# First stage of a decoder step: memory values first, high halves and row sums on ScalarE, statistics through a diagonal, four shared weight slots

## The reference

```python
def _rmsnorm(x, g):
    xf = x.astype(jnp.float32)
    y = xf * lax.rsqrt(jnp.mean(xf * xf, axis=-1, keepdims=True) + RMS_EPS)
    return (y * g.astype(jnp.float32)).astype(x.dtype)

def _mem_kv(mem, g, w_k, w_v):
    n, m, _ = mem.shape
    hm = _rmsnorm(mem, g)
    return ((hm @ w_k).reshape(n, m, MEM_HEADS, MEM_HEAD_DIM),
            (hm @ w_v).reshape(n, m, MEM_HEADS, MEM_HEAD_DIM))
...
mkv = [_mem_kv(mem_prompt, norm_mem_kv[l], mem_w_k[l], mem_w_v[l]) for l in range(DEPTH)]
...
h = _rmsnorm(x, norm_mix[0])
u = h @ pool_w_in[0]
u_ext = u if pool_buf is None else jnp.concatenate([pool_buf[0], u], axis=1)
```

## Time and profile before

| what | value |
|---|---|
| median of three runs | 2504.84 us (2499.56 to 2507.42) |
| profiled execution, span on the core | 2500.6 us (no other total is given for it) |
| TensorE busy | 2411.1 us (96%) |
| VectorE, ScalarE, GpSimd busy | 1435.8, 820.9, 236.0 us |
| DMA | 433 MB, mean 173 GB/s |
| first matmul of `win` | 159.84 us |

### The profile page before, as it was taken

How to read it: one execution, slowest core, us unless ns; L and a number is a source line. 1 busy time by engine, 2 the same in 40 slices (tenths; PEclk the granted TensorE clock), 3 DMA queues, 4 the chain that set the end, 5 groups by cost and what they waited for, 6 DMA issues and landing times.

```text
span 2500.6 us, 45442 instructions
## 1 busy us (share of the span) xinstructions
PE 2411.1 (96%) x19126; PEld 2336.1 (93%) x19126; DVE 1435.8 (57%) x1419; ACT 820.9 (33%) x593; POOL 236.0 (9%) x230
## 2 busy tenths in 40 slices
PE   5989999899999999999999999998999999999998
PEld 5879997899999999999988997968999999999998
DVE  8587776755544554455655762847545445544555
ACT  3323433133333333333332332323333333333332
POOL 7040021200000000000201012312000000000002
PEclk7999999999999999999999999999999999999999
DMA  4745557155555556555445455454555555565553
GB/s 141 222 162 176 186 169 261 60 185 178 191 172 177 189 168 194 176 168 183 170 169 165 136 188 188 152 185 136 168 187 182 177 180 180 170 200 168 170 183 119
DMA packets 374185, 433.27 MB, mean 173 GB/s; under 512 B 7954, under 2 KB 340066, under 8 KB 373552
## 3 DMA queue, kind: packets, MB, share of 16 engines
q1 hardware_dynamic: 363632, 394.51, 48.2%
q0 software_dynamic: 10160, 36.83, 4.3%
q10 hardware_dynamic: 288, 0.43, 0.1%
HBM read 426.21 MB, written 6.45 MB: 173 GB/s over the span
## 4 chain that ended last, share of the span: by engine, by line
PE 54%; issue 34%; DVE 5%; POOLq 2%; DMA 2%; DVEq 2%; ACT 0%; POOL 0%; SPq 0%; ACTq 0%
PE acc L621 16%; PE acc L623 16%; PE acc L622 16%; DVE wlo L1075 1%; DVE xs L1113 1%; POOLq L1605 1%; PE acc L707 1%; POOLq L1600 1%; DVEq L1114 1%; PE ab L768 1%; DVE xs L1116 1%; PE ab L883 1%; DMA xs_flat<-in_cache_mem_k 1%; DMA raw<-in_mem_w_v 1%; PE acc L697 1%
## 5 line engine op out<-in xcount | busy, mean ns | idle before, releaser
L621 PE MATMUL acc<-xs,whi 128*128 128x264 f32 (+1 forms) x3712 | 1069.2, 288 | 37.2 <-DVE xs L1116 11.5
L623 PE MATMUL acc<-xs,wlo 128*128 128x264 f32 (+1 forms) x3712 | 1060.5, 286 | 0.0
L622 PE MATMUL acc<-xs,whi 128*128 128x264 f32 (+1 forms) x3712 | 1059.5, 285 | 0.0
L416 ACT ACTIVATE whi<-raw 128x2048 fp32r<-128x2048 f32 x372 | 706.9, 1913 | 1065.1 <-DMA raw<-in_ffn_w_up 304.0
L1075 DVE TENSOR_TENSOR wlo<-raw,whi 128x2048 fp32r<-128x2048 f32 x372 | 848.1, 2309 | 265.9 <-ACT whi L416 190.9
L621 PEld LDWEIGHTS acc<-xs,whi 128*128 128x128 f32 x3712 | 702.2, 189 | 41.0 <-issue 15.2
L623 PEld LDWEIGHTS acc<-xs,wlo 128*128 128x128 f32 x3712 | 706.5, 190 | 0.0
L622 PEld LDWEIGHTS acc<-xs,whi 128*128 128x128 f32 x3712 | 704.2, 190 | 0.2
L621 PE MATMUL acc<-hA,whi 128*128 128x264 f32 (+1 forms) x1216 | 350.2, 288 | 15.6 <-DVE x L1122 9.5
L623 PE MATMUL acc<-hA,wlo 128*128 128x264 f32 (+1 forms) x1216 | 348.6, 287 | 0.0
L622 PE MATMUL acc<-hA,whi 128*128 128x264 f32 (+1 forms) x1216 | 348.0, 286 | 0.0
(11 more groups left out here) (210 smaller groups left out, 1517.4 us busy)
## 6 DMA issues: line engine op xcount, KB each, us to landing
raw<-in_ffn_w_gate SPq DMA_DIRECT2D x88, 1024.0 KB, 5.3
raw<-in_ffn_w_up SPq DMA_DIRECT2D x88, 1024.0 KB, 5.2
raw<-in_ffn_w_down SPq DMA_DIRECT2D x88, 1024.0 KB, 5.4
raw<-in_dil_w_q SPq DMA_DIRECT2D x24, 1024.0 KB, 5.0
raw<-in_pool_w_in SPq DMA_DIRECT2D x16, 1024.0 KB, 5.5
raw<-in_pool_w_out SPq DMA_DIRECT2D x16, 1024.0 KB, 5.7
raw<-in_mem_w_k SPq DMA_DIRECT2D x8, 1024.0 KB, 5.3
raw<-in_mem_w_v SPq DMA_DIRECT2D x8, 1024.0 KB, 5.5
```

What stands on the lines that cost most here:

```text
L416: nc.scalar.activation(whi[:, n % NSPLIT, :], raw[:, n % 2, :], ACT.Copy).then_inc(hi_ready, 1)
L621: mm(out, w_hi, hi_, start=first, stop=False)
L622: mm(out, w_hi, lo_, start=False, stop=False)
L623: return mm(out, w_lo, hi_, start=False, stop=last)
```

## The change

What it does, part by part:

- Order of phases on TensorE: values of layer 0, then the transposes of token and state rows, keys 0, values 1, transposes of keys 0, keys 1, transposes of keys 1, `win`. In `value_phase` the loop over channel tiles is outside and the two token groups inside, so that a tile is used as soon as it is there.
- ScalarE makes the high halves of the normed inputs (`high_x`), VectorE only the low ones (`low_x`, `low_memory`). GpSimd makes none, and no squares before `wout`.
- ScalarE sums the squares of the memory and token rows as they lie, tokens on partitions (`rows_sum`). VectorE puts the sums on a diagonal (`diagonals`), and TensorE multiplies it by ones, which gives the sums along the free dimension (`row_statistics`).
- The transposed memory has a buffer of its own (`memT` in `kx`), no longer `x`. SP loads the token and state rows behind the first four blocks, into buffers outside `xs`; identity and gains are issued by ScalarE.
- `raw` has four slots and the low half is written over it in place (`wlo` is another name of the same memory). SP loads a block when TensorE has used the block four earlier. `hi` and `lo` no longer wait for that themselves.

```diff
-    ("memk0", 4, 2), ("memv0", 4, 1), ("memkt0", 0, 1),
-    ("memk1", 4, 2), ("xt", 0, 5), ("st", 0, 2), ("memv1", 4, 1), ("memkt1", 0, 1),
+    ("memv0", 4, 1), ("xt", 0, 5), ("st", 0, 2),
+    ("memk0", 4, 2), ("memv1", 4, 1), ("memkt0", 0, 1), ("memk1", 4, 2), ("memkt1", 0, 1),
...
-        raw = sb("raw", [P, 2, BLK])
         whi = sb("whi", [P, NSPLIT, BLK], F32R)
-        wlo = sb("wlo", [P, NSPLIT, BLK], F32R)
+        with nc.sbuf_tensor("wlo", [P, NSPLIT, BLK], F32R) as wlo:
+            pass
+        raw = sb("raw", [P, NSPLIT, BLK])
...
-                if n >= 2:
-                    eng.wait_ge(hi_ready, n - 1)
-                    eng.wait_ge(lo_ready, n - 1)
+                if n >= NSPLIT:
+                    eng.wait_ge(half_used, 2 * (n - NSPLIT + 1))
                 src = weight_source(n)
-                eng.dma_start(raw_as(n % 2, src.shape[1]), src).then_inc(raw_in[n % 2], 16)
+                eng.dma_start(raw_as(n % NSPLIT, src.shape[1]), src).then_inc(raw_in[n % NSPLIT], 16)
...
+                if n == NSPLIT:
+                    for key in (("x", 0), ("x", 1), ("x", 2), ("state", 0)):
+                        load_cached(eng, key)
...
                 landed(eng, n, more)
-                if n >= NSPLIT:
-                    eng.wait_ge(half_used, more * 2 + 2 * (n - NSPLIT + 1))
-                nc.scalar.activation(whi[:, n % NSPLIT, :], raw[:, n % 2, :], ACT.Copy).then_inc(hi_ready, 1)
+                nc.scalar.activation(whi[:, n % NSPLIT, :], raw[:, n % NSPLIT, :], ACT.Copy).then_inc(hi_ready, 1)
...
+            def rows_sum(key, c):
+
+                cached_landed(eng, key)
+                if c:
+                    eng.wait_ge(rows_summed, c)
+                nc.scalar.activation(ab[:, :, :].rearrange("p b c -> p (b c)"), cached(key), ACT.Square,
+                                     accum_out=ssqc[:, c:c + 1]).then_inc(rows_summed, 1)
+
+            def high_x(gen, m, src, width):
+
+                c = GAIN[gen[:-1]][0 if gen == "memkv0" else int(gen[-1])] + m
+                return nc.scalar.activation(xs[:, m, 0, 0:width], src, ACT.Copy, scale=gains[:, c:c + 1]).then_inc(xhi_ready, 1)
...
-            upto(1)
+            for c in range(2):
+                rows_sum(("mem", c), c)
+            hi(0)
+            at[0] = 1
             eng.wait_ge(acc_free, G0["xload"] + 1)
+            for m in range(DC):
+                high_x("memkv0", m, memT[:, m, :], TP)
+                if m % 4 == 3 and m < 12:
+                    upto(1 + m // 4)
...
+            root(STAT["mem"], TP)
+            eng.wait_ge(rows_summed, 2)
+            nc.scalar.activation(stdc[:, 0:2], ssqc[:, 0:2], ACT.Sqrt, bias=eps[:, :], scale=1.0 / D).then_inc(std_ready, 1)
+            upto(N0["memk0"])
             for m in range(DC):
...
-                if m % 8 == 3:
-                    upto(2 + m // 8)
-            root(STAT["mem"], TP, 2)
+            eng.wait_ge(std_ready, STAT["mem"] + 1)
+            for c in range(2):
+                rows_sum(("x", c), 2 + c)
+            upto(N0["memk0"] + 3)
+            upto(N0["memv1"])
+            eng.wait_ge(half_used, 2 * (N0["memk0"] + 4))
+            for m in range(DC):
+                high_x("mix0", m, x[:, m, :], T)
+                if m % 4 == 3 and m < 12:
+                    upto(N0["memv1"] + 1 + m // 4)
...
-                    for c in range(3 if samples else 2):
-                        out, t0, tn = (acc[:, 2 * (g % 2) + c, :], c * P, P) if c < 2 else (acc[0:TS, 2 * ((g + 1) % 2), :], TP, TS)
-                        for k in range(4):
+                    for k in range(4):
+                        if ready is not None:
+                            ready(4 * i + k)
+                        for c in range(3 if samples else 2):
+                            out, t0, tn = (acc[:, 2 * (g % 2) + c, :], c * P, P) if c < 2 else (acc[0:TS, 2 * ((g + 1) % 2), :], TP, TS)
...
-                        if c == 0 or c == (2 if samples else 1):
+                        if k % 2 == 1:
                             last.then_inc(half_used, 1)
...
+            def row_statistics(k, d, samples):
+
+                eng.wait_ge(diag_ready, d)
+                for c in range(2):
+                    last = mm(ab[:, 3, c * P:(c + 1) * P], ones[:, :], sq_flat[:, c * P:(c + 1) * P], start=True, stop=True)
...
-            pair_item(N0["memk0"], G0["memk0"], 2, xtile, xs_wait("memkv0"), width=TP)
-            statistics(STAT["mem"], TP, 2)
-            pair_item(N0["memk0"] + 2, G0["memk0"] + 1, 2, xtile, width=TP)
...
-            value_phase("memv0", False)
-            memory_keys_out(0)
-            pair_phase("memk1", 2, 2, htile, lambda k: eng.wait_ge(low_ready, k // 2 + 1), TP)
+            value_phase("memv0", False, None, xs_wait("memkv0"), lambda: row_statistics(STAT["mem"], 1, False))
...
-            value_phase("memv1", False, htile)
+            pair_phase("memk0", 2, 2, xtile, width=TP)
+            value_phase("memv1", False, htile, lambda k: eng.wait_ge(low_ready, k + 1))
+            memory_keys_out(0)
+            pair_phase("memk1", 2, 2, htile, width=TP)
             memory_keys_out(1)
-            pair_phase("win", 8, 2, xtile, xs_wait("mix0"), after_first=lambda: statistics(STAT["mix0"]))
+            pair_phase("win", 8, 2, xtile, xs_wait("mix0"), after_first=lambda: row_statistics(STAT["mix0"], 2, True))
...

-                landed(eng, n, more)
                 eng.wait_ge(hi_ready, more + (n + 1))
-                if n >= NSPLIT:
-                    eng.wait_ge(half_used, more * 2 + 2 * (n - NSPLIT + 1))
-                v.tensor_tensor(wlo[:, n % NSPLIT, :], raw[:, n % 2, :], whi[:, n % NSPLIT, :].bitcast(F32),
+                v.tensor_tensor(wlo[:, n % NSPLIT, :], raw[:, n % NSPLIT, :], whi[:, n % NSPLIT, :].bitcast(F32),
                                 ALU.subtract).then_inc(lo_ready, 1)
...
-            for m in range(0, DC, 2):
-                split_x(GAIN["memkv"][0], m, TP)
-                if m in (0, 6):
-                    upto(m // 6)
-            upto(3)
-            rms(STAT["mem"], TP, 2)
...
+            def low_x(gen, m, src, width):
+
+                c = GAIN[gen[:-1]][0 if gen == "memkv0" else int(gen[-1])] + m
+                eng.wait_ge(xhi_ready, 16 * XHI[gen] + m + 1)
+                v.scalar_tensor_tensor(out=xs[:, m, 1, 0:width], in0=src, scalar=gains[:, c:c + 1],
+                                       in1=xs[:, m, 0, 0:width].bitcast(F32), op0=ALU.mult, op1=ALU.subtract).then_inc(xs_ready, 1)
...
+            def diagonals(c0):
+
+                eng.wait_ge(rows_summed, c0 + 2)
+                for c in range(2):
+                    last = v.tensor_scalar(sq_flat[:, c * P:(c + 1) * P], ident[:, :], ssqc[:, c0 + c:c0 + c + 1], None, ALU.mult)
+                return last
...
+            eng.wait_ge(ident_in, 16)
+            lo(0)
+            at[0] = 1
+            for m in range(DC):
+                low_x("memkv0", m, memT[:, m, :], TP)
+                if m == 1:
+                    diagonals(0).then_inc(diag_ready, 1)
+                if m in (3, 7, 11):
+                    upto(1 + m // 4)
+            rms(STAT["mem"], TP, 2)
+            upto(N0["memk0"])
+            for m in range(10):
+                low_memory(m)
             memory_values(0)
-            upto(N0["memk1"] + 3)
-            memory_keys(1, N0["memv1"])
...
+            upto(N0["memk0"] + 1)
...
+            upto(N0["memk0"] + 2)
+            eng.wait_ge(stat_ready, STAT["mem"])
+            diagonals(2)
...
+            v.tensor_reduce(ssq[:, 0, 0:TS], squares.rearrange("p m b -> p b m"), AX.X, ALU.add).then_inc(diag_ready, 1)
+            for m in range(10, DC):
+                low_memory(m)
+            memory_keys(0, 0)
+            upto(N0["memk0"] + 3)
+            upto(N0["memv1"])
+            memory_keys(0, 1)
+            for m in range(DC):
+                low_x("mix0", m, x[:, m, :], T)
+                if m in (3, 7, 11):
+                    upto(N0["memv1"] + 1 + m // 4)
+            upto(N0["memk1"])
             memory_values(1)
+            upto(N0["memk1"] + 1)
+            memory_keys_staged(0)
...
-            squares(lambda j: taken(G0["memload"] + 3), TP)
-            taken(G0["xload"])
-            for m in range(0, DC, 2):
-                h, k, c = (hA, hB)[m // 8], m % 8, GAIN["memkv"][1] + m
...
-                eng.wait_ge(high_ready, m + 2)
-                gp.tensor_tensor(h[:, k:k + 2, 1, 0:TP], sq[:, :, 0:TP], h[:, k:k + 2, 0, 0:TP].bitcast(F32),
-                                 ALU.subtract).then_inc(low_ready, 1)
-                eng.drain()
-            load_cached(eng, ("x", 0))
-            load_cached(eng, ("x", 1))
-            eng.wait_ge(half_used, 2 * N0["memk1"])
-            for key in (("x", 2), ("state", 0)):
-                load_cached(eng, key)
-            squares(lambda j: taken(G0["xt"] + 4))
+            taken(G0["memkt0"])
```

(9 more changed lines are left out.)

123 lines of the change are left out of this document (69 added, 54 removed).

## The result

The kernel after takes 2457.83 us (median of 4, 2456.69 to 2459.17) against 2504.03 us (median of 4, 2499.56 to 2507.42) for the kernel before on the same chip: a ratio of 0.9821, 95% interval 0.9807 to 0.9835, so 46 us less. The forecast was 2468; its direction and main term held, and the time came out 10 us lower, 0.8 us above the lower end of the range of 2457 to 2487.

The account below looks back on a forecast made before the run. TensorE was taken as the bound, busy 2411.1 of 2500.6 us, with the first stage loose behind VectorE. The median 2504.84 less 37.1 us there, slots 0, gave 2467.7, say 2468; range 2457 to 2487.

Parts of the forecast that it names:

- main term: First stage, up to the first evacuation of the input projection: 137.3 us against 174.4, 37.1 us less.
- Start of the values: First values matmul on TensorE: at 18.0 us, not 20.8; 18.3 or 16.5 by other readings of DMA issue.
- Values of layer 0: First values phase: 22.4 us at full pace plus 2.5 for a slow clock spell and row statistics, ending at 42.9.
- Turning step: Transposing token and state rows between layer 0's values and keys: 10.0 us on VectorE, ending at 52.9.
- The ten megabytes of the sum: Data landing through the first keys block: 10 MB at 350 GB/s, landing near 33 us.
- rival A: Rows late: first keys block lands at 38 us, not 33, some 6 us lost, 2474 us; chance 0.20.
- Keys, values 1, keys 1: Rest of the first stage: keys 22.8 us each, values 22.4 + 0.3, input projection from 124.9, first evacuated at 137.3.
- GpSimd: First stage: losing its squares and second low halves gains nothing itself, but its absence allows VectorE's 2.29 and 0.45 us.
- Four slots: Weight loads in the loops: taken as 0; bounds 3 us gained and 6 us lost beside cache loads.
- From profile to median: Whole time: the three-run median lies 4.2 us above the profiled span, carried over to the forecast.
- Rival D: Better: start at 16.5 us, no slow clock spell, loops gain 3 us, 2461 us; chance 0.09.
- C: Slower: four slots make weights late in the steady loops, 2521 us at an excess of 0.6 us; chance 0.05.

Follow-up runs that it names:

- gains_on_sync: Kernel after, with the identity and seven gain rows issued by SyncE among the memory rows again, as before; 2459.68 us.
- pool_busy: Kernel after, with a hundred added multiplications of 384 columns on GpSimd from the start, ahead of the mask's load; 2474.94 us.
- layer1_first: Kernel after, with sixteen high and ten low tiles of the second layer's memory moved ahead of the first keys block; 2456.46 us, repeated 2454.79.
- after_again: Kernel after, unchanged, measured again beside later candidates on the same chip; 2457.18 us.
- slots_only: Kernel before, with the four shared weight slots alone; 2488.90 us, 0.9941 of before.
- two_raw_rest: Kernel after, with weight blocks from the window projection on landing in two slots again, with the old waits; 2468.97 us.

## Why the prediction was right, and what it missed

- **Start of the values**: 18.0 forecast, 16.91 measured, inside the bounds 16.5 to 18.3. That earlier issue is nearly worthless was right: 0.72 of 3.83 us in gains_on_sync, against the 0.3 taken. The first high half nevertheless came 1.65 us earlier than the earlier trace rows has it; 0.87 of that is not explained by the issue and was not tried apart.
- **Values of layer 0**: 24.9 us forecast, 24.4 measured (16.91 to 41.32), with a slow spell as counted: granted clock 0.69 from 16 to 20 us and 0.88 from 20 to 24.
- **Turning step**: 10.0 us forecast, 12.8 measured (41.3 to 54.16). This step failed in its mechanism. The sum watched the second keys block; it was the first, landing at 35.88 and not 33, with low tiles behind it in VectorE's order that the evacuation had to wait for. The ten megabytes of the sum leave out the mask (0.4 MB), which is asked for ahead of that block, and from 24 to 32 us the DMA engines, with a share of 1.05, moved 267 GB/s and not the 350 of the sum; in pool_busy, where the mask comes later, the block lands at 33.34, at a rate that is no better there (244 GB/s). That points to the mask, but no run moved it alone. It is rival A at under half of its price; layer1_first takes 2.5 us of wait away. 0.9 us of the 12.8 belong to a spell of low clock (granted clock 0.83 from 40 to 50 us; eight transposes take 1.97 us at 45.45, in layer1_first 1.09); in after_again, without it and with the block at 35.20, the step takes 10.2 us (42.33 to 52.53).
- **Keys, values 1, keys 1**: the last item of the keys of layer 0 is evacuated at 77.12, 23.0 us after their start (22.8 forecast). The first window eviction is at 138.77 for 137.3; in after_again it is at 137.15.
- **GpSimd**: its absence was rightly said to stand above the 2.29 and 0.45. A GpSimd that works without a break to 126.9 us costs the first stage 17.4 us. How much of the 35.6 us goes back to GpSimd's shorter work in the kernel before was not measured. High tiles on ScalarE are 5.3, the slots 3.1, the order of the phases none. These were changed one at a time and need not add; what is left was not separated, among it the tokens' splits beside the second values phase: the 9.93 us hole of the earlier trace rows is gone, and the longest wait of TensorE from 60 to 138 us is 0.79, but no run moved them alone.
- **Four slots**: the mis-sized term, 0 taken with 3 us gained as the bound; measured 8.7 us (slots_only) and 9.6 (two_raw_rest) in the rest, 6.0 to 6.3 us in one product. The prediction priced what a late refill can cost and saw the gain only where the feed-forward starts. It overlooked the case in which VectorE itself is the late one: there a landing slot held by its low half makes a loop of load, high half, low half and addition. It also read TensorE's idle share as an average of 1.7% from 300 to 2400 us; in the down product it was 5.8% (3.92 of 68.00 us), with gaps at its third and fourth pair of additions. The Trainium skill's rule that the prediction cites on consistent bubbles and missing buffers ("Perfetto Trace Analysis", section "Optimization Strategy") would have pointed there if the rows had been cut by stage. The runs agree with it as far as landing slots go: with four of them the gaps are gone, with fewer slots in all (four for six).
- **From profile to median**: 4.2 us were carried over from before; after has 0.8 between its profiled span and its median. The profiled execution of after (span 2457.0, time 2459.17) was the slowest of its four. The nine executions of before beside the last experiments have spans from 2497.0 to 2508.2, four of them below the profiled 2500.6. So this term is the spread of single executions, and its part in the sum is chance.
- The sum of the errors: 1.5 us too much gain in the stage, 8.0 too little in the rest, 3.4 in the offset, which gives the 9.9 us between 2467.7 and 2457.83. Rival D had the loops gain 3 us and 2461; C, the only way to slower, is contradicted in its sign: no wait of TensorE in the feed-forward loops of after ends with a late block.

## What to carry to other kernels

When a buffer is handed back by an engine that also does bursts of other work, its hand-back time is that engine's worst stretch, not its mean; tie the refill to the last reader instead and give it more slots (the two were not tried apart), and look for the gain in the stretch where the burst is. Read idle shares stage by stage: an average of 1.7% hid a product with 5.8%. In an in-order queue, put work whose inputs are there ahead of work that waits for a load, even where the load's result is needed first; here that took a wait of 3.10 us to 0.63, and the time moved by less than could be told.

## What was not expected of the hardware

Beside GpSimd instructions of 384 columns (pool_busy), a VectorE instruction with two SBUF inputs mostly took about 0.6 us longer, nearly whatever its own length (0.41 to 0.98, 2.29 to 2.91), so many short instructions suffer most: 16 low tiles lose 9.1 us where four low halves lose 2.5. Beside GpSimd's 512 columns in the kernel before it took 0.83 longer, again at both lengths: 2.54 for a pair of 256 columns where the kernel after takes 0.87 (43.20), and 3.12 for a low half in place of 2.29. The price went with the length of GpSimd's instruction (384 to 512 is 0.75, 0.6 to 0.83 is 0.72), as far as two lengths can show.

```profile
17.48 3.12 DVE L1075 TENSOR_TENSOR wlo<-raw,whi 128x2048 fp32r<-128x2048 f32 x1
```

In the other direction, an addition of 1.3 us on GpSimd took 3.13 beside that low half:

```profile
16.01 1.26 POOL L1602 TENSOR_TENSOR ssq<-ssq,sq 128x512 f32<-128x512 f32 x1
...
18.60 3.13 POOL L1602 TENSOR_TENSOR ssq<-ssq,sq 128x512 f32<-128x512 f32 x1
```
